# A transformer block with product-key experts on one Trainium2 core: the second norm beside the output projection, query weights loaded earlier, and three row buffers instead of four for the first 32 rows

## The reference

```python
x = x + mixed @ w_out[l]
x = x + peer_ffn(rms_norm(x, norm2_g[l]), peer_w_query[l], peer_sub_keys[l], peer_down[l], peer_up[l])

def peer_ffn(xn, w_query, sub_keys, expert_down, expert_up):
    ...
    qry = (xt @ w_query).reshape(T, PEER_HEADS, 2, PEER_QDIM // 2)
    sc = jnp.einsum('thcd,hckd->thck', qry.astype(f32), sub_keys.astype(f32))
    top_s, top_i = lax.top_k(sc, PEER_TOPK)
    kk = PEER_TOPK * PEER_TOPK
    cand_s = (top_s[:, :, 0, :, None] + top_s[:, :, 1, None, :]).reshape(T, PEER_HEADS, kk)
    ...
```

## Time and profile before

| | us |
|---|---|
| median of 3 runs | 2331.84 |
| lowest and highest | 2329.73, 2332.44 |
| profiled execution, its own time | 2329.87 |
| its span in the trace | 2328.1 |
| PE busy | 2056.1 (88%) |
| DVE busy | 1299.4 (56%) |
| ACT busy | 814.3 (35%) |
| POOL busy | 260.3 (11%) |

### The profile page before, as it was taken

The page is one execution under the profiler, slowest core; times in us unless marked ns, Lnnn a source line. Parts: engine busy times, 40 slices in busy tenths (PEclk is TensorE's granted clock), DMA queues, the critical chain, the costliest instruction groups (busy, mean ns, idle before and its releaser), DMA issues. The chain is left out here.

```text
span 2328.1 us, 21752 instructions
## 1 busy us (share of the span) xinstructions
PE 2056.1 (88%) x8141; PEld 1333.8 (57%) x8141; DVE 1299.4 (56%) x2001; ACT 814.3 (35%) x1737; POOL 260.3 (11%) x267
## 2 busy tenths in 40 slices
PE   6999999997989889977777898899877799999997
PEld 5878778772444444422323344444322798999886
DVE  5545665445654555545566555556644666475555
ACT  5446564412212212212222322122121655355454
POOL 0000000002121211112112111111211000000000
PEclk9999999999999999989999999999999999999999
DMA  5545556469999999999999999999999656466662
GB/s 211 163 135 164 162 176 209 166 284 429 427 428 428 427 428 427 426 426 414 428 428 428 427 427 424 426 427 425 413 428 405 202 146 187 123 203 200 185 195 80
DMA packets 87513, 729.90 MB, mean 314 GB/s; under 512 B 10192, under 2 KB 10320, under 8 KB 51696
## 3 DMA queue, kind: packets, MB, share of 16 engines
q0 software_dynamic: 36864, 536.89, 54.4%
q1 hardware_dynamic: 50544, 191.63, 25.5%
HBM read 724.28 MB, written 4.19 MB: 313 GB/s over the span
## 5 line engine op out<-in xcount | busy, mean ns | idle before, releaser
L1318 PE MATMUL bank<-ring,work 128*128 128x512 f32 x2048 | 962.9, 614 | 205.9 <-ACT work L1396 202.9
L1551 DVE CUSTOM_DVE_ANT_0 ring<-ring,mix_t 128x2048 f32<-128x2048 f32 x256 | 586.9, 2293 | 551.9 <-DMA ring<-in_peer_rows_dram,work 549.7
L1318 PEld LDWEIGHTS bank<-ring,work 128*128 128x128 f32 x2048 | 374.6, 192 | 726.2 <-issue 380.7
L487 DVE TENSOR_TENSOR ring_r<-ring,ring_r 128x1024 fp32r<-128x1024 f32 (+2 forms) x300 | 334.5, 1145 | 304.5 <-ACT ring_r L466 303.9
L1459 POOL DMA_INDIRECT ring<-in_peer_rows_dram,work x256 | 256.3, 1001 | 1511.8 <-PE bank L1318 965.2
L1392 ACT ACTIVATE work<-work 128x1 f32<-128x1 f32 x256 | 52.4, 205 | 958.9 <-DVE work L1551 958.8
L520 PE MATMUL bank<-ring_r,mix_r 128*128 128x512 f32 (+1 forms) x1184 | 374.6, 391 | 0.0
L466 ACT ACTIVATE ring_r<-ring 128x1024 fp32r<-128x1024 f32 (+2 forms) x300 | 288.5, 992 | 168.4 <-DMA ring<-in_w_out_dram 52.0
L520 PE MATMUL bank<-ring_r,act_r 128*128 128x512 f32 (+1 forms) x736 | 269.1, 387 | 0.0
L520 PEld LDWEIGHTS bank<-ring_r,mix_r 128*128 128x128 f32 x1184 | 220.3, 189 | 42.1 <-issue 1.8
L517 PE MATMUL bank<-mix_r,ring_r 128*128 128x256 f32 (+1 forms) x1216 | 227.4, 289 | 7.7 <-DVE ring_r L487 7.7
(11 more groups left out here) (372 smaller groups left out, 1252.1 us busy)
## 6 DMA issues: line engine op xcount, KB each, us to landing
ring<-in_w_in_dil_dram SPq DMA_DIRECT2D x72, 512.0 KB, 3.6
ring<-in_w_out_dram SPq DMA_DIRECT2D x64, 512.0 KB, 3.6
ring<-in_w_in_mo_dram SPq DMA_DIRECT2D x48, 384.0 KB, 3.6
h<-in_w_query_dram SPq DMA_DIRECT2D x8, 2048.0 KB, 11.8
ring<-in_w_in_gla_dram SPq DMA_DIRECT2D x24, 512.0 KB, 3.6
ring<-in_w_in_ml_oz_dram SPq DMA_DIRECT2D x24, 512.0 KB, 3.8
h<-in_xa_wkv_dram SPq DMA_DIRECT2D x4, 2048.0 KB, 21.3
ring<-in_w_in_lru_dram SPq DMA_DIRECT2D x16, 512.0 KB, 3.6
```

Of the source, the lines that this page charges most:

```text
L487: dve.tensor_tensor(low(c), raw(c), plain(high(c)), ALU.subtract).then_inc(k.weights_low, 1)
L1318: m = pe.matmul(B[c][:, :], diag[:, d % 2, :], slots[:, d % DEPTH, 1, c * 512:(c + 1) * 512], start=first, stop=last)
L1551: dve.tensor_tensor_reduce(row, row, xn[:, t, :], 1.0, 0.0, ALU.mult, ALU.add, dots[:, p, j:j + 1]) \
```

## The change

- **The second norm moves beside the projection.** `norm2_beside` turns the unscaled residual: blocks 0 and 1 (16 transposes) after chunks 5 and 6 of the second pair, blocks 2 and 3 (16 more) behind the last chunk. The factor 1/rms (`rstd`) is made meanwhile and put in afterwards, as the scale of the copies that stage the scores, and in the product with the gain that makes `xn`. The stage `normalise` for norm2 is gone. The high parts of `out1`'s input move from `act_r` to `mix_r`, so that `act3` is free to be written.
- **Order of the lead-in on PE.** The scores of head 0 for the first 128 tokens are put after 6 of 16 matmuls of the part that follows. Head 2's query leaves the lead-in and is made in pieces beside unit 0's rows.
- **Query weights.** Heads 2 and 3 get rooms of their own: head 2 in `mem_kv` and in the place of the gain, head 3 in the fourth row buffer. Head 3 is loaded at once as the stage starts, head 2 once `xn` is made, heads 4 and 5 once heads 0 and 1 are made. Every load is issued as two halves.
- **Row buffers.** Rows 0 to 31 go round three buffers. Row 32 takes the fourth, and waits for `query_done` >= 4, the query of head 3; from there on all four are used.

The diff, cut:

```diff
--- before.py
+++ after.py
...
+    def out_hi(self, at):
+        return self.mix_r[:, at.start - GLA_H:at.stop - GLA_H, :]
+    def out_lo(self, at):
+        if at.start < 2 * GLA_H:
+            return self.mix_r[:, at.start + 2 * GLA_H:at.stop + 2 * GLA_H, :]
+        return self.act_r[:, at, :]
...
+def norm2_beside(k, mem, beside, stream, out1, rstd, name="norm2"):
...
+    first, end = stream.at(out1, 2), len(stream.chunks)
+    TICKS = [(first + 5) / PER_TICK, (first + 6) / PER_TICK, end / PER_TICK, end / PER_TICK + 1]
+    turn_at = lambda kc: B[kc // 2 % 4][:, kc % 2 * T:(kc % 2 + 1) * T]
+    def tensor(pe):
+        for b, tick in enumerate(TICKS):
+            yield tick
+            pe.wait_ge(*stream.out(out1, b))
+            if b >= 2:
+                pe.wait_ge(taken_act, 2 * (b - 1))
+                pe.wait_ge(taken_dve, 2 * (b - 1))
+            for kc in range(4 * b, 4 * b + 4):
+                for t in range(NT):
+                    m = pe.transpose(turn_at(kc)[:, t * P:(t + 1) * P], k.x3[:, t, kc * P:(kc + 1) * P], k.c("ident"))
+                if kc % 2:
+                    m.then_inc(turned, 1)
+    def scalar(act):
+        for b, tick in enumerate(TICKS):
+            yield tick
+            if b == 3:
+                act.wait_ge(meaned, 1)
+                act.activation(mem.sd, mem.ms, ACT.Sqrt).then_inc(rooted, 1)
+            act.wait_ge(turned, 2 * b + 1)
+            for kc in (4 * b, 4 * b + 1):
+                act.activation(k.act3[:, kc, :], turn_at(kc), ACT.Copy, scale=gain[:, kc:kc + 1]).then_inc(taken_act, 1)
+    def vector(dve):
+        for b, tick in enumerate(TICKS):
+            yield tick
+            dve.wait_ge(turned, 2 * b + 2)
+            for kc in (4 * b + 2, 4 * b + 3):
+                dve.tensor_scalar(k.act3[:, kc, :], turn_at(kc), gain[:, kc:kc + 1], None, ALU.mult).then_inc(taken_dve, 1)
+            if b == 2:
+                dve.wait_ge(k.squared, NT * 4)
+                dve.tensor_reduce(mem.sd, k.sums3, AX.X, ALU.add).then_inc(own, 1)
+                dve.wait_ge(own, 1)
+                dve.tensor_scalar(mem.ms, mem.sd, 1.0 / D, EPS, ALU.mult, ALU.add).then_inc(meaned, 1)
+        dve.wait_ge(rooted, 1)
+        dve.reciprocal(rstd, mem.sd).then_inc(inverted, 1)
...
+    norm2_beside(k, mem, beside, stream, out1, rstd)
     project(k, stream, "in1", split_act, beside=beside, junk=shaped(k.work[:, 1024:5120], NT, 4, 512))
...
+FOUR_FROM = 2 * PEER_TOP
+def row_buffer(d):
+    return d % 3 if d < FOUR_FROM else (3, 2, 0, 1)[(d - FOUR_FROM) % 4]
...
+def row_before(d):
+    return next((e for e in range(d - 1, -1, -1) if row_buffer(e) == row_buffer(d)), None)
...
+def query_room(head):
+    if head < 4:
+        return head, 1
+    return head % 2, head // 2
+def query_before(head):
+    return head - 4 if head < 6 else head - 2
+def query_piece(k, room, kc):
+    half = KC // 2
+    if room == 3:
+        at = k.ring[:, 3 * 2 * D + kc // half * 2048:3 * 2 * D + kc // half * 2048 + 2048]
+    elif room < 2:
+        at = k.h[:, room * 4096 + kc // half * 2048:room * 4096 + kc // half * 2048 + 2048]
+    else:
+        at = k.h[:, 10240:12288] if kc >= half else k.mem_kv[:, :]
+    return shaped(at, half, 2 * PEER_K)
+
 def load_query(sp, k, head, loaded):
 
     w = k.ins["w_query"][head] if head < PEER_H else k.ins["xa_wkv"][head - PEER_H]
-    sp.dma_start(shaped(k.h[:, (head % 2) * 4096:(head % 2 + 1) * 4096], KC, 2 * PEER_K), w) \
-      .then_inc(loaded[head % 2], 16)
-
-
-def peer(k, query_in, keys_in, gain_in, name="peer"):
+    room, _ = query_room(head)
+    half = KC // 2
+    for kc in (0, half):
+        sp.dma_start(query_piece(k, room, kc), w[:, kc:kc + half, :]).then_inc(loaded[room], 16)
...
-            for head in range(2, PEER_H):
-                sp.wait_ge(query_done, head - 1)
+            load_query(sp, k, 3, query_in)
+            sp.wait_ge(gained, NT)
+            load_query(sp, k, 2, query_in)
+            for head in range(4, PEER_H):
+                sp.wait_ge(query_done, query_before(head) + 1)
                 load_query(sp, k, head, query_in)
             sp.wait_ge(scored, PEER_H)
-            sp.wait_ge(gained, NT)
             sp.dma_start(mem, ins["mem"].rearrange("(t p) d -> p t d", p=P)).then_inc(mem_in, 16)
             for head in range(KV0, KV1):
-                sp.wait_ge(query_done, head - 1)
+                sp.wait_ge(query_done, query_before(head) + 1)
...
-            pe.wait_ge(query_in[0], 16)
-            for f in range(2):
-                first_tokens(f, 0, B[4 + f][:, 0:P]).then_inc(first_query, 1)
+            pe.wait_ge(*query_there(0))
+            first_tokens(0, 0, B[4][:, 0:P]).then_inc(first_query, 1)
+            first_tokens(1, 0, B[5][:, 0:P], range(6))
             pe.wait_ge(keys_in, 16)
             first_score(0)
-            first_tokens(0, 1, B[0][:, 0:P])
+            first_tokens(1, 0, B[5][:, 0:P], range(6, KC)).then_inc(first_query, 1)
+            first_tokens(0, 1, B[0][:, 0:P], range(6))
             first_score(1)
+            first_tokens(0, 1, B[0][:, 0:P], range(6, KC))
             first_tokens(1, 1, B[0][:, P:2 * P]).then_inc(query_done, 1)
             pe.wait_ge(query_out, 1)
             for c in range(2):
@@ -1345,18 +1458,16 @@
             query(1, 1, range(KC))
             pe.wait_ge(staged_done, 1)
             score(1, 1)
-            query(2, 0, range(KC))
-            score(2, 0)
             for n in range(UNITS):
                 for j in range(K):
-                    if 0 < n < PEER_H - 2:
+                    if n < PEER_H - 2:
                         query(n + 2, n % 2, [j])
                     if n == PEER_H + 1 and j % 2 == 0:
                         turn_memory(j // 2)
                     if 0 <= n - PEER_H - 2 < KV1 - KV0:
                         query(n - 2, n % 2, [j], of_memory=True)
                     add_row(n, j)
-                if 0 < n < PEER_H - 2:
+                if n < PEER_H - 2:
                     score(n + 2, n % 2)
...
+                    act.activation(flat(staged[:, p, :, :]), B[6 + p][:, 0:256], ACT.Copy, scale=rstd[:, 0:1]).then_inc(staged_done, 1)
+                    act.activation(later[:, n, :], B[6 + p][:, 256:512], ACT.Copy, scale=rstd[:, 1:2]).then_inc(stored, 1)
...
             gate(0, 0)
-            take_query(2, 0)
...
-                if n + 2 < PEER_H and n:
+                if n + 2 < PEER_H:
...
-                    if d >= DEPTH:
-                        pool.wait_ge(added, d - DEPTH + 1)
+                    if row_before(d) is not None:
+                        pool.wait_ge(added, row_before(d) + 1)
+                    elif row_buffer(d) == 3:
+                        pool.wait_ge(query_done, 4)
                     pool.nop(nofuse=True)
-                    pool.indirect_dma_start(slots[:, d % DEPTH, :, :].rearrange("p a b -> p (a b)"), None, ins["peer_rows"],
+                    pool.indirect_dma_start(slots[:, row_buffer(d), :, :].rearrange("p a b -> p (a b)"), None, ins["peer_rows"],
                                             bass.IndirectOffsetOnAxis(ap=rows[:, n % 2, j:j + 1], axis=0)) \
-                        .then_inc(row_in[d % DEPTH], 16)
+                        .then_inc(row_in[row_buffer(d)], 16)
...
-                dve.tensor_tensor(xn[:, t, :], xn[:, t, :], gain, ALU.mult).then_inc(gained, 1)
+                dve.scalar_tensor_tensor(xn[:, t, :], k.x3[:, t, :], rstd[:, t:t + 1], gain, ALU.mult, ALU.mult).then_inc(gained, 1)
...
-        normalise(k, "norm2", k.x3, k.c("norm2_g"), k.act3, summed=True)
-        peer(k, query_in, keys_in, gain_in)
+        rstd = k.work[:, 6142:6144]
+        query_in, keys_in, gain_in = first_block(k, split_act, from_act, residual, rstd)
+        peer(k, query_in, keys_in, gain_in, rstd)
```

More of the change, by code:

```diff
@@ L526, in _, with normalise @@
             rest(len(chunks) // PER_TICK)
-def normalise(k, name, src3, gain, dst3, load=None, upcoming=None, late=None, summed=False):
+def normalise(k, name, src3, gain, dst3, load=None, upcoming=None, late=None):
     nc = k.nc
@@ L575, in _ @@
                 dve.wait_ge(arrived, 32)
[L576 to L582, removed]
+            dve.tensor_tensor_reduce(xs[:, 1, :], src3[:, 1, :], src3[:, 1, :], 1.0, 0.0, ALU.mult, ALU.add, ms[:, 1:2]) \
+               .then_inc(own_squared, 1)
+            dve.wait_ge(squared, 1)
             dve.wait_ge(own_squared, 1)
@@ L1111, in scalar_high @@
             act.wait_ge(mixed, h + 1)
-            act.activation(mem.act_hi[:, 4 + h, :], mix_bank(h), ACT.Copy).then_inc(high, 1)
+            act.activation(flat(mem.out_hi(slice(GLA_H + h, GLA_H + h + 1))), mix_bank(h), ACT.Copy).then_inc(high, 1)
     def scalar_exp(act):
@@ L1135, in dilated_beside @@
     return low, stored
-def first_block(k, split_act, from_act, residual):
+def norm2_beside(k, mem, beside, stream, out1, rstd, name="norm2"):
+    B, gain = k.banks, k.c("norm2_g")
```

(19 more changed lines are left out.)

44 lines of the change are left out of this document (23 added, 21 removed).

## The result

The changed kernel takes **2357.01 us** in the median of 4 runs (2355.71 to 2361.85), the kernel before 2330.78 beside it (4 runs). The ratio is 1.0116, with an interval of 1.0098 to 1.0133: slower by 26.2 us, where +14.3 was forecast, and 3.0 above the upper end of the range given (2333 to 2354). The profiled execution took 2356.52 with a span of 2354.7, which is 26.6 more than the span before.

What follows compares the result with a forecast made beforehand. Row stage bound by bytes through DMA; three buffers too few. Row 32 comes 19.2 us later, less 4.9 for one load, +14.3: 2329.87 becomes 2344.2, or 2346.2 by the runs' median; 2345 given, range 2333 to 2354.

Steps and rivals of the forecast that it cites:

- the two holes: DMA share 0.00 in the kernel before, from 434 to 476 and near 518, the second while PE makes head 2's query.
- the lead-in up to dot 0: Projection's end to first dot: query starts 3.4 us earlier, at 458.7, and dot 0 at 491.4.
- row 32's wait for head 3's query: Row 32 waits for the query's last piece behind row 30's add, goes out at 673.9 and lands at 683.4, 19.2 later.
- The projection did not stall: Rival in the projection: PE's transposes and DVE's scalings hold each other up, some 8 us more, 2353; chance 0.08.
- The rival of three sufficient buffers: Row stage: a gather costs 7.0, the cycle 14.84, nearly DMA's 14.67, so a gain to 2316; chance 0.13.
- The even pattern of 4.9, 4.9 and 7.6: Sign for gathers 3 to 31: spacings within a period of 17.4 us per three rows.
- the 0.82 to 0.88 given as a sign: Sign: DMA share expected between 510 and 665, while rows go round three buffers.
- The first add then comes 3.4 later: Unit 0, after dot 0: dot of 2.29 and three small ACT steps, so first add at 494.8, not 511.32.
- A buffer therefore can't be reused faster than 9.54 + 7.06 + 0.78 = 17.38 us.: Rows 3 to 31: issue to landing, landing to add's end, next issue; three buffers give 5.79 us a row.
- the 8.8 that I gave as the lower end: Shorter issue to landing of an unqueued gather: period 16.64, time 2336 to 2338; chance 0.17.
- The stretch after row 32 loses one load of 2.1 MB, 4.9 us.: Behind row 32: head 5's weights load earlier, at 488.7, which takes 4.9 us off the delay.
- My turning point was 8.24: Issue to landing, counted eleven times in the sum: at 8.24 us the change turns from loss to gain.

Runs made afterwards that it cites:

- e2: Kernel before with only the row buffers changed: rows 0 to 31 go round three, with no wait for a query; 2366.49 us, ratio 1.0151.
- e1: Changed kernel with four row buffers for all 256 rows, head 3's weights loading into head 1's room; 2318.78 us, ratio 0.9946 to the kernel before.
- e6: Changed kernel with one more 128x512 matmul on PE behind each add of units 0 and 1; 2353.65 us in one run.
- e5: Changed kernel with the dots of rows 3 to 31 cut to the first 64 of 2048 columns; 2334.72 us in one run.
- e7: Changed kernel, dots of rows 3 to 31 except 16 replaced by a 64-column dot and three PSUM copies; 2347.15 us in one run.
- e3: Changed kernel with three row buffers for all 256 rows; 2587.03 us in one run.

## Why the prediction came out as it did

**Right.** That the row stage is bytes; that three buffers can't keep DMA full, the two holes, the lead-in up to dot 0, and row 32's wait for head 3's query: from row 30's landing to row 32's I had 18.2, measured 18.07. The projection did not stall: it ended 3.9 later, for 2.7 forecast. The rival of three sufficient buffers fell with e2. The even pattern of 4.9, 4.9 and 7.6 did not come: rows 3 to 30 stood 4.9 to 7.8 apart in no fixed order, and the DMA share was 0.90 to 0.91, above the 0.82 to 0.88 given as a sign.

**Sizes that were off.** At row 32 the change is 28.8 behind, where I had 19.2. Three terms make the 9.6, and a fourth stands after it:
- *"The first add then comes 3.4 later (...), at 494.8".* It came 1.9 later: 0.6 of it the dot's own delay, 1.28 a table load on ACT that the sum did not have. And it took 5.40. Because the gather then ran in 8.0, row 3 landed only 2.1 late (510.87 for 508.8).
- *"A buffer therefore can't be reused faster than 9.54 + 7.06 + 0.78 = 17.38 us."* This step failed: the period was 18.24, +0.86, 7.7 us in nine. Of the 0.86, 0.30 lies between issue and landing and 0.55 on the way back. I took one row's 9.54 for the price of an empty queue, and used it both as least and as mean. The least is 8.0, under the 8.8 that I gave as the lower end, and the mean in this loop 9.84, since queueing and late landings come on top. The way back, 7.84, holds only while adds take 3.7: PE idles between the spread-out rows, its granted clock is 0.91 and 0.94 in the mean of the two stretches (1.00 in e1) and 0.50 in short parts of them (514 to 517, 528 to 531, 545 to 548), and single adds take 5.1 to 5.4. The mean was 8.39. With the clock held up by the filler (e6) it was 8.07, but the period stayed at 18.11, so what the clock costs in time is not shown.
- *From row 30 to row 32:* -0.1.
- *"The stretch after row 32 loses one load of 2.1 MB, 4.9 us."* It did: the change is 28.81 behind at row 32 and 23.92 at row 34. But 2.5 were lost again by row 38 (26.39), which the sum had at nothing: behind the long wait the add of row 32 starts at 696.48 and takes 6.26, gather 36 goes out only at 703.52, and DMA moves 347 GB/s from 705 to 710. At the end 26.6 are left, so 2.2 in all came back.

Together 2.1 + 7.7 - 0.1 + 2.7 = 12.4, and 14.3 + 12.4 = 26.7, which is the 26.6 measured.

The direction rested on 9.54 more than I knew, and that 9.54 lies near the mean of the loop, 9.84, was luck. My turning point was 8.24, and the least measured is under it: had I known 8.0 and used it alone, the period would have been 15.84 and the forecast a gain. This loop did not run at the sum of its parts' least times: 18.24 was measured, not 15.84.

## What to carry to other kernels

A ring of buffers needs its number times the transfer time to exceed the whole cycle of one buffer, with room to spare: four buffers at 19.6 for a cycle of at least 15.8 kept DMA full (428 GB/s), three at 14.7 did not (350). Even in e5, where the least values add up to 13.9, three buffers moved only 360 to 401. Take the cycle's parts from several records in the state that the change will make, and look at what stands beside each; and keep a buffer in the ring rather than park weights in it, where the stage is bound by bytes. A bundle of edits should be run apart: here 12 us of gain lay under 38 of loss.

## What the runs showed of the hardware

- A gather's issue on POOL, 0.94 long, that starts inside a dot (2.29 us, two SBUF operands) lasts until 0.80 to 0.83 after the dot's end: 34 of 39 in the change, up to 2.97 long. Four of the other five started in a dot's last 0.15, one 0.02 behind its start. Beside copies that read PSUM no issue was held (e7); beside a DVE instruction with one large SBUF operand one was (2.22).
- A 2.1 MB gather into an empty queue lands 7.7 to 8.3 after its issue in the undisturbed cases (8.01 for gather 3 of the change, 7.70 at the least, gather 55 of e3), and up to 3 us later in others (gather 18 of the change by 2.91); behind a full queue rows land 4.90 apart with a lateness of about 0.01 (e1).
- Packets of 16 KB take 0.61. Over 0.9 took 8 to 9 in 100 in the loop of three buffers, 0.2 to 0.4 in 100 with a full queue (e1). So a DMA share of 0.90 went with 350 GB/s, where 1.00 went with 428.
- In rows 3 to 30 of the change the eight adds of 5.1 to 5.4 us in place of 3.6 to 3.7 stood behind a wait of 2.0 to 3.3 us on PE; of the other twenty, one stood behind 2.2 and the rest behind 1.8 or less. With one filler matmul per row (e6) the clock of the two stretches was 0.98 and 1.00, without it 0.91 and 0.94.
